# Adding the gate biases of the second layer on VectorE instead of through two short matmuls

## The reference, cut to what matters

```python
h = rms_norm_2(x, mix_norm_pre[l]) * (1.0 + sc1) + sh1
a_q, a_f, a_i, a_g, b_q, b_k, b_v, c_a, c_g = split_cols_2(h @ w_in[l], IN_SPLITS)
ya = hgrn2_mixer(a_q, a_f, a_i, a_g, lower_bounds[l], hgrn_norm_w[l])
yb = dilated_attention_mixer(b_q, b_k, b_v, rel_bias)
yc = conv_module(c_a, c_g, conv_w[l], conv_b[l], conv_ln_g[l], conv_ln_b[l])
gates = jax.nn.sigmoid(h @ w_gate[l] + b_gate[l]).reshape(Bsz, S, N_BRANCH, D)
merged = (gates[:, :, 0] * (ya @ w_a_out[l]) + gates[:, :, 1] * (yb @ w_b_out[l])
          + gates[:, :, 2] * (yc @ w_c_out[l]))
x = x + g1 * rms_norm_2(merged @ w_o[l], mix_norm_post[l])
```

## Time and profile before

| | |
|---|---|
| median of 3 runs | 3223.1 us (3222.22 to 3224.41) |
| the profiled execution: span from first to last instruction | 3220.3 us |
| what lies around the span, against the median | 2.8 us |
| PE busy | 3075.7 us (96%) |
| DVE busy | 2066.5 us (64%) |
| ACT busy | 1513.0 us (47%) |
| mean granted TensorE clock | 0.979 |
| the stage `second_mixers` | about 1530 to 2440 us of the span |
| gate blocks 16 to 27 on PE | about 1920 to 2260 us |

### The profile page before, as it was taken

How to read it: one execution, slowest core, us unless ns; L and a number is a source line. 1 busy time by engine, 2 the same in 40 slices (tenths; PEclk the granted TensorE clock), 3 DMA queues, 4 the chain that set the end, 5 groups by cost and what they waited for, 6 DMA issues and landing times. The chain is left out here.

```text
span 3220.3 us, 43840 instructions
## 1 busy us (share of the span) xinstructions
PE 3075.7 (96%) x17864; PEld 2446.1 (76%) x17864; DVE 2066.5 (64%) x2332; ACT 1513.0 (47%) x1822; POOL 20.1 (1%) x10
## 2 busy tenths in 40 slices
PE   8999978998899999999999989999997999999997
PEld 7888855966787776666688878877776888888885
DVE  5557547365868787785558868755666556555555
ACT  4345432143656566563444475555444444444443
POOL 0000001000000000000000000000000000000000
PEclk9999978999999999999999999999999999999998
DMA  7979868087978788793576654575766555555551
GB/s 265 337 262 341 288 212 338 4 303 293 342 270 321 264 295 306 254 345 131 160 234 209 225 180 148 191 245 167 267 209 231 174 183 184 190 186 183 187 189 68
DMA packets 358321, 739.09 MB, mean 230 GB/s; under 512 B 19977, under 2 KB 118422, under 8 KB 344583
## 3 DMA queue, kind: packets, MB, share of 16 engines
q1 hardware_dynamic: 342916, 711.64, 64.3%
q10 hardware_dynamic: 15236, 25.06, 2.1%
HBM read 710.00 MB, written 26.65 MB: 229 GB/s over the span
## 5 line engine op out<-in xcount | busy, mean ns | idle before, releaser
L286 DVE TENSOR_TENSOR moe_w_lo<-ring,moe_w_hi 128x1024 fp32r<-128x1024 f32 x384 | 461.5, 1221 | 163.7 <-ACT moe_w_hi L276 156.2
L276 ACT CAST moe_w_hi<-ring 128x1024 fp32r<-128x1024 f32 x384 | 402.3, 1049 | 277.6 <-PE psum L302 274.5
L286 DVE TENSOR_TENSOR mx_w_lo<-ring,mx_w_hi 128x1024 fp32r<-128x1024 f32 (+1 forms) x288 | 347.1, 1210 | 281.8 <-ACT mx_w_hi L276 277.8
L286 DVE TENSOR_TENSOR mlp_w_lo<-ring,mlp_w_hi 128x1024 fp32r<-128x1024 f32 x256 | 313.5, 1225 | 293.3 <-ACT mlp_w_hi L276 292.2
L276 ACT CAST mx_w_hi<-ring 128x1024 fp32r<-128x1024 f32 (+1 forms) x288 | 297.1, 1038 | 424.2 <-PE psum L302 409.2
L276 ACT CAST mlp_w_hi<-ring 128x1024 fp32r<-128x1024 f32 x256 | 268.4, 1049 | 418.0 <-PE psum L302 418.0
L302 PE MATMUL psum<-mx_w_hi,mx_a_hi 128*128 128x496 f32 (+1 forms) x1024 | 405.8, 396 | 6.8 <-DVE mx_w_lo L286 4.9
L302 PE MATMUL psum<-mx_w_lo,mx_a_hi 128*128 128x496 f32 (+1 forms) x1024 | 398.1, 389 | 0.0
L302 PE MATMUL psum<-mx_w_hi,mx_a_lo 128*128 128x496 f32 (+1 forms) x1024 | 397.9, 389 | 0.0
L286 DVE TENSOR_TENSOR in_w_lo<-ring,in_w_hi 128x628 fp32r<-128x628 f32 x192 | 155.3, 813 | 185.5 <-ACT in_w_hi L276 184.3
L302 PE MATMUL psum<-in_w_hi,in_a_hi 128*128 128x314 f32 x768 | 244.1, 318 | 1.7 <-DVE in_w_lo L286 1.2
(11 more groups left out here) (604 smaller groups left out, 5582.8 us busy)
## 6 DMA issues: line engine op xcount, KB each, us to landing
ring<-in_w_ada SPq DMA_DIRECT2D x72, 1024.0 KB, 9.1
ring<-in_w_e_gate SPq DMA_DIRECT2D x64, 1024.0 KB, 5.5
ring<-in_w_e_up SPq DMA_DIRECT2D x64, 1024.0 KB, 6.3
ring<-in_w_e_down SPq DMA_DIRECT2D x64, 1024.0 KB, 5.2
ring<-in_w_up SPq DMA_DIRECT2D x64, 1024.0 KB, 5.2
ring<-in_w_down SPq DMA_DIRECT2D x64, 1024.0 KB, 5.1
ring<-in_w_in SPq DMA_DIRECT2D x64, 992.0 KB, 5.1
ring<-in_w_in SPq DMA_DIRECT2D x96, 628.0 KB, 5.5
```

The source lines that it names most:

```text
L276: self.nc.scalar.copy(self.w[0][:, self._half(j, half), :, 0:cols], self.view[:, slot, ks, 0:cols]).then_inc(self.hi_done, 1)
L286: self.nc.vector.tensor_tensor(self.w[1][:, q, :, 0:cols], self.view[:, j % self.slots, ks, 0:cols], self.w[0][:, q, :, 0:cols].bitcast(F3 ...
```

## The change

The two matmuls, `ones2`, `braw`, `bias2` and their waits go. SP fetches the bias row of a block into all 128 partitions of `b_row`, which has two places. When a gate block is finished, DVE adds the row to both token tiles on its way from PSUM to `out` (`add_bias`); ACT takes the sigmoid in place in `out` and waits for DVE. The PSUM pair is free when DVE has added.

```diff
-        braw, bias2, ones2 = st.sb("braw", [33, NB]), st.sb("bias2", [33, NB], F32R), st.sb("ones2", [33, P], F32R)
+        b_row = st.sb("b_row", [P, 2, NB])
...
 (SP)
                     if c == 0 and 0 <= g < GATES:
-                        sp.wait_ge(b_lo, g + 1)
-                        for r in (0, 32):
-                            sp.dma_start(braw[r:r + 1], d["b_gate_2"][:, g * NB:(g + 1) * NB]).then_inc(b_in, 16)
+                        if g >= 2:
+                            sp.wait_ge(biased, g - 1)
+                        sp.dma_start(b_row[:, g % 2], d["b_gate_2"][0, g * NB:(g + 1) * NB].partition_broadcast(P)).then_inc(b_in, 16)
...
 (PE)
                     if c == half == 0 and n >= 2:
-                        pe.wait_ge(evicted, n - 1)
+                        if n - 2 < n_in:
+                            pe.wait_ge(evicted, n - 1)
+                        else:
+                            pe.wait_ge(biased, n - 1 - n_in)
...
-                    if c == half == 0 and gate:
-                        pe.wait_ge(b_lo, n - n_in + 2)
-                        for t in range(T):
-                            mm = nc.tensor.matmul(to(t), ones2[:], bias2[:], start=True, stop=False)
-                        mm.then_inc(b_used, 1)
...
 (ACT, evict; the sigmoid of a gate block)
-                        nc.scalar.activation(out[:, n % 2], bank[:, pair(n)], ACT.Sigmoid).then_inc(evicted, 1)
+                        sc.wait_ge(biased, n - n_in + 1)
+                        nc.scalar.activation(out[:, n % 2], out[:, n % 2], ACT.Sigmoid).then_inc(evicted, 1)
...
-                nc.scalar.copy(ones2[:], chip.c("ones")[0:33, :]).then_inc(b_hi, 1)
...
-                        if c == 1 and half == 0 and 0 <= g < GATES:
-                            sc.wait_ge(b_in, 32 * (g + 1))
-                            if g:
-                                sc.wait_ge(b_used, g)
-                            nc.scalar.copy(bias2[:], braw[:]).then_inc(b_hi, 1)
...
 (DVE)
-                nc.vector.memset(braw[:], 0.0).then_inc(b_lo, 1)
+                def add_bias(j, n):
+                    g = n - n_in
+                    split.done(ve, j)
+                    ve.wait_ge(stored[n % 2], 16 * (n // 2))
+                    ve.wait_ge(b_in, 16 * (g + 1))
+                    nc.vector.tensor_tensor(out[:, n % 2], bank[:, pair(n)], over(b_row[:, g % 2], 1, T),
+                                            ALU.add).then_inc(biased, 1)
...
                         if j + 2 < body:
                             split.lo_half(ve, j + 2, half, 0, cols(j + 2))
-                        if c == 2 and half == 0 and 0 <= g < GATES:
-                            ve.wait_ge(b_hi, g + 2)
-                            nc.vector.tensor_tensor(bias2[32:33], braw[32:33], bias2[32:33].bitcast(F32),
-                                                    ALU.subtract).then_inc(b_lo, 1)
+                        if c == KC - 1 and half == 1 and n_in <= n < ABC0:
+                            add_bias(j, n)
```

More of the change, by code:

```diff
@@ L2697, in second_mixers @@
         rooms.work = early.enter_context(nc.sbuf_tensor("mx_work", [P, n_work], F32))
-        evicted, b_in, b_hi, b_lo, b_used = (st.sem(n) for n in ("evicted", "b_in", "b_hi", "b_lo", "b_used"))
+        evicted, b_in, biased = (st.sem(n) for n in ("evicted", "b_in", "biased"))
         stored = [st.sem(f"stored{n}") for n in range(2)]
@@ L2756, in stream @@
                 def stream(j, n, c, half):
-                    gate, width = n >= n_in, cols(j)
+                    width = cols(j)
                     to = lambda t: bank[:, pair(n).start + t, 0:width]
                     if c == half == 0 and n >= 2:
-                        pe.wait_ge(evicted, n - 1)
+                        if n - 2 < n_in:
+                            pe.wait_ge(evicted, n - 1)
+                        else:
+                            pe.wait_ge(biased, n - 1 - n_in)
                     if n == 0 and half == 0:
                         pe.wait_ge(split.act_lo, c + 1)
-                    if c == half == 0 and gate:
-                        pe.wait_ge(b_lo, n - n_in + 2)
-                        for t in range(T):
-                            mm = nc.tensor.matmul(to(t), ones2[:], bias2[:], start=True, stop=False)
-                        mm.then_inc(b_used, 1)
-                    split.use_half(pe, j, half, to, split.parts, c * KC, c == half == 0 and not gate,
-                                   c == KC - 1 and half == 1, width)
+                    split.use_half(pe, j, half, to, split.parts, c * KC, c == half == 0, c == KC - 1 and half == 1,
+                                   width)
                 def product(j, i, q, half):
@@ L2834, in evict @@
                 def evict(j, n):
-                    split.done(sc, j)
-                    if n >= 2:
-                        sc.wait_ge(stored[n % 2], 16 * (n // 2))
                     if n < n_in:
+                        split.done(sc, j)
+                        if n >= 2:
+                            sc.wait_ge(stored[n % 2], 16 * (n // 2))
                         nc.scalar.copy(out[:, n % 2, :, 0:W2], bank[:, pair(n), 0:W2]).then_inc(evicted, 1)
                     else:
-                        nc.scalar.activation(out[:, n % 2], bank[:, pair(n)], ACT.Sigmoid).then_inc(evicted, 1)
+                        sc.wait_ge(biased, n - n_in + 1)
+                        nc.scalar.activation(out[:, n % 2], out[:, n % 2], ACT.Sigmoid).then_inc(evicted, 1)
                 def square(b):
@@ L2857, in _ @@
                     n, c = divmod(j, KC)
-                    g = n - n_in + 1
                     for half in range(2):
@@ L2916, in _ @@
                     n, c = divmod(j, KC)
-                    g, i = n - n_in + 1, n - ABC0
+                    i = n - ABC0
                     for half in range(2):
```

## The result

The changed kernel takes 3232.2 us (median of 6 runs, 3230.8 to 3238.2), the kernel before 3222.8 in the runs beside it: ratio 1.0031, 95% interval 1.0020 to 1.0042. It is slower by 9.4 us where I had 3223.4 and a range up to 3231. A second measurement gave 3229.0 against 3222.3, ratio 1.0015 (1.0005 to 1.0025; the two medians alone would give 1.0021). Both intervals lie above 1, so the kernel is slower; how much is uncertain by some us.

What follows compares the result with a forecast made beforehand. PE was taken as the bound, busy throughout the gate blocks. Savings from removed matmuls and delays from the DVE-to-ACT chain summed to +0.3 us on a span of 3220.3; with 2.8 more for the median, 3223.4, range 3216.5 to 3231.

Steps and rivals of the forecast that it cites:

- Head: Stage's start: DVE's memset of braw ahead of the norm goes and moves the stage up, -0.41 us.
- Block 16: PE's 1.43 us wait for the bias goes, but the gain is given back by 1926.83; 0 (bounds 0 and -2.3).
- Levels: Four block ends at a level's start: PE's L2326 waits for the later ACT and DVE queues, together +2.7 us.
- A free block: Gate block end with enough slack, as at half 184: the removed bias matmul pair saves PE 0.87 us.
- Half 191: ACT's attention exponential stands behind the later sigmoid, so PE's L2567 starts later: +0.57 us in place of -0.87.
- Half 223: ACT's copy L2611 stands a half behind the sigmoid: between 0 and +1.11 us, taken as +0.1.
- Rival 3: DVE gets 6.4 us more busy time in 340 and fills up, showing as L302 waiting for L286; no chance given.
- half 199: Attention: ACT's copy L2611 stands behind the later sigmoid and PE has no slack, +1.11 us in place of a saving.
- rival 1: Slower: six new PE waits cost clock, 1.73 us each, +10.4 if all fall; chance of over +6.4 us: 0.15.
- Zero to three falls: Clock falls at 1.7 us each allowed on top of the sum, within the 3220 to 3229 held at 0.75.
- three signs of being wrong: L2326 waits at none of four places, clock at 0.50 behind most new waits, or PE waits for L286.
- Rival 2: Faster: engines have more slack, all twelve pairs, wait and head kept, -12.3 us, 3210.8; chance of over 6.4 us: 0.10.

## Why the prediction was wrong

*The mechanics held.* Without clock, my steps add up to +0.8 us where I had +0.3:

- Head: -0.41, measured -0.48, the memset's length.
- Block 16: 0, measured 0. The wait of 1.43 is gone, and three waits of L302 for L286 came in its place (0.72, 0.40 and 0.81 us at halves 128 to 130), with DVE waiting for ACT as foretold.
- Levels: +2.7, measured +3.4. L2457 starts 6.03 us behind the low part in the earlier trace rows and 7.20 after: 1.17, not 1.11. And the 32 matmuls take 3.84 us where they have to wait for DVE, 3.74 where they have not the earlier trace rows. That is 0.16 for each of four.
- A free block: -0.87, as measured. (By the rule of the Trainium skill, "TensorE: Matmul & The Clock Gate", section Back-to-back issue gap, the pair is estimated at 0.43; these blocks decide for the trace.)
- Half 191: +0.57, measured +0.50. Halves 202 to 224: -1.33, measured -1.32. Half 223: +0.1, measured +0.26.
- Rival 3 made no wait of L302 for L286 behind the first add, but DVE's fill decided where the add could be moved to.

*The step that failed* is the pricing of the clock, in half 199 of the sum and in rival 1. At 199 the delay was 1.1, as foretold, but the stretch there was 2.05 us and not 1.7 (0.87 of the pair and 1.11 are 1.98 already), and behind it PE ran at 0.51 for 6.5 us: 6.5 x 0.49 = 3.2 us in place of the 1.73 that I took for a fall from the earlier trace rows. The sum itself had nothing for clock. Moving one sigmoid took this loss away, and so did filling the wait.

Then I looked for lost clock only behind new waits. The stretch of 2.62 at the convolution is in both kernels, but the head that is 0.48 shorter moved it to where the clock fell; that term (+1.5) was in no case of mine. The product blocks got another 0.5 net. There the old wait at L2033 grew from 2.77 to 3.74 us, one of 0.81 at L302 went, and the low clock behind lasted longer; I have not separated these. So 4.7 of the 6.1 us are clock (3.2 and 1.5), and part of the last 0.5 may be.

"Zero to three falls" at 1.7 each had room for that, up to 3229; the 2.7 us ahead of the stage put the profiled run above it, and the median lies beyond my range. How much of the median's 9.4 comes from there stays open: the two measurements of this kernel differ by 1.6 in 1000.

None of my three signs of being wrong came: L2326 waited at all four places, one new wait of six had the low clock behind it, and PE waited for L286 only in block 16, ahead of the first add. They did not cover what went wrong.

*Rival 1* named the right mechanism and the wrong test. Only one of six new waits lost clock, yet "on the side of 1.43 or of 1.89" is no property of a wait: the same 1.43 kept the clock in one kernel and lost it in another, the same 2.62 too. *Rival 2* had its slack denied: the removal alone gave 3.9, not 12.3. Two slips of the working change nothing: half of rival 2 is 3217.0 and not 3216.5, and 6.4 us in 340 would bring DVE to 85.5 and not 85.3 in 100 (it measured 84.67).

## What to carry to other kernels

An instruction taken from the bound engine is worth its time only where nothing else is due just behind it; look up which block ends meet a due time, and put what the change adds at the tail of the queue there, or where the engine that gets it is idle. Price each idle stretch of PE of some 1.4 us and more (the shortest here with a low clock behind it was 1.43) with a chance of a slow clock of its own, old ones as well, since any shift ahead of them deals these anew. A difference of 1 to 3 us between two schedules may be that deal alone: read the clock behind each wait in both traces before the instructions are given the credit.

## What the runs showed of the hardware

Idle stretches of 1.43 us and 2.62 us each came both with and without a low clock behind them; for the 2.62 a shift of 0.48 us far ahead decided it. The loss behind one stretch of 2.05 us was 3.2 us in one schedule and about 1.6 in another. A table load on ACT ran ahead of the wait of its activation (load at 1959.29, wait of 1.13 us, activation at 1961.70). Sixteen fp32 matmuls of 128 x 128 x 128 are 32 in the trace, 0.114 us each.
